# Attention layer: squares folded in two, one ones-product per sum of squares, the norm chain and the last score pairs a slot later

## The reference, cut to what matters

```python
def rms_norm(x, g):
    xf = x.astype(jnp.float32)
    y = xf * lax.rsqrt(jnp.mean(xf * xf, axis=-1, keepdims=True) + EPS)
    return (y * g.astype(jnp.float32)).astype(x.dtype)
...
    q = rms_norm(q, q_norm_g[:, None, :])
    k = rms_norm(k, k_norm_g[:, None, :])
    ...
    q, k = partial_rope(q, cos, sin), partial_rope(k, cos, sin)
```

## Time and profile before

| | |
|---|---|
| median of 3 runs | 2274.46 us (2269.77 to 2276.57) |
| the profiled execution, its own time | 2273.7 us |
| its span, first to last instruction | 2272.0 us |
| busy over the span: PE, PEld | 2232.2 us (98%), 1869.4 us (82%) |
| busy over the span: DVE, ACT, POOL | 1395.7 us (61%), 1231.3 us (54%), 398.0 us (18%) |
| mean granted clock of TensorE | 0.998 |
| attention heads | about 1081 to 2187 us of the span; from the second on, the scaled copies of one head start 137.5 us after those of the head before |
| weight loads of the attention heads | 80 of 512 KB, median 3.9 us from issue to landing |

### The profile page before, as it was taken

How to read it: one execution, slowest core, us unless ns; L and a number is a source line. 1 busy time by engine, 2 the same in 40 slices (tenths; PEclk the granted TensorE clock), 3 DMA queues, 4 the chain that set the end, 5 groups by cost and what they waited for, 6 DMA issues and landing times. The chain is left out here.

```text
span 2272.0 us, 31343 instructions
## 1 busy us (share of the span) xinstructions
PE 2232.2 (98%) x11056; PEld 1869.4 (82%) x11056; DVE 1395.7 (61%) x2594; ACT 1231.3 (54%) x2509; POOL 398.0 (18%) x672
## 2 busy tenths in 40 slices
PE   7999999999999999999999999999999999999999
PEld 5788888888888888777888888888888888888887
DVE  5867758585867665586745738366482755728451
ACT  5656656566666665555545455454555545455440
POOL 2435162533525160560000000000000000000000
PEclk9999999999999999999999999999999999999999
DMA  4212231322222245586111121121111211121241
GB/s 144 56 45 65 72 84 46 82 47 71 50 68 61 59 106 179 189 264 202 56 38 57 29 57 47 38 65 39 48 38 40 64 47 40 37 64 49 92 175 60
DMA packets 301726, 174.26 MB, mean 77 GB/s; under 512 B 97228, under 2 KB 284004, under 8 KB 301572
## 3 DMA queue, kind: packets, MB, share of 16 engines
q1 hardware_dynamic: 301572, 172.26, 26.6%
HBM read 143.66 MB, written 28.56 MB: 76 GB/s over the span
## 5 line engine op out<-in xcount | busy, mean ns | idle before, releaser
L390 PE MATMUL b_front<-g_h_lo,wa_w_hi 128*128 128x512 f32 x2064 | 827.3, 401 | 0.0
L390 PE MATMUL b_front<-g_h_hi,wa_w_hi 128*128 128x512 f32 x2064 | 821.9, 398 | 5.4 <-PEq L1563 3.0
L390 PE MATMUL b_front<-g_h_hi,wa_w_lo 128*128 128x512 f32 x2064 | 823.9, 399 | 0.0
L390 PEld LDWEIGHTS b_front<-g_h_hi,wa_w_hi 128*128 128x128 f32 x2064 | 388.6, 188 | 82.5 <-issue 6.2
L390 PEld LDWEIGHTS b_front<-g_h_lo,wa_w_hi 128*128 128x128 f32 x2064 | 388.5, 188 | 76.7 <-issue 0.2
L390 PEld LDWEIGHTS b_front<-g_h_hi,wa_w_lo 128*128 128x128 f32 x2064 | 388.4, 188 | 76.1 <-issue 0.5
L2215 ACT ACTIVATE b_acc<-b_front,g_gains 128x512 f32<-128x512 f32 x96 | 66.2, 689 | 300.3 <-DVE p_qk L2534 201.1
L1287 DVE SCALAR_TENSOR_TENSOR a_acc<-a_x_raw,a_hw,a_acc 128x512 f32<-128x512 f32 x192 | 156.9, 817 | 6.6
L2405 DVE TENSOR_TENSOR wa_w_lo<-wa_raw,wa_w_hi 128x1024 fp32r<-128x1024 f32 x79 | 95.6, 1210 | 106.2 <-ACT wa_w_hi L2161 106.2
L779 POOL TENSOR_TENSOR a_bt<-a_bd,a_bx 128x112 f32<-128x112 f32 (+29 forms) x248 | 116.7, 471 | 213.7 <-DMA a_bd<-u_tiles 194.9
L782 POOL TENSOR_TENSOR a_bx<-a_bx,a_bt 128x112 f32<-128x112 f32 (+29 forms) x248 | 131.4, 530 | 19.4
(11 more groups left out here) (355 smaller groups left out, 4074.0 us busy)
## 6 DMA issues: line engine op xcount, KB each, us to landing
wa_raw<-in_b_w_in_dram SPq DMA_DIRECT2D x80, 512.0 KB, 3.9
wa_raw<-in_a_w_in_dram SPq DMA_DIRECT2D x48, 512.0 KB, 4.5
p_w_raw<-in_a_w_out_dram SPq DMA_DIRECT2D x40, 512.0 KB, 4.1
a_out<-a_og SPq DMA_DIRECT2D x64, 128.0 KB, 1.9
a_zx<-inverse_tiles SPq DMA_DIRECT2D x16, 384.0 KB, 4.4
p_a_raw<-a_out SPq DMA_DIRECT2D x40, 128.0 KB, 4.9
u_tiles<-a_u SPq DMA_DIRECT2D x8, 512.0 KB, 3.2
a_bd<-u_tiles SPq DMA_DIRECT2D x32, 128.0 KB, 3.6
```

Source lines behind the costliest of these rows:

```text
L390: last = pe.matmul(out, w[:, k, :], a[:, k, ks], start=(n == 0), stop=(n == 23))
```

## The change

The squares of the lower 64 dimensions stay where they were (`sg`), those of the upper 64 are written to the lower partitions of a second buffer (`sq_up`); DVE adds the two, so 64 rows of sums of two squares are left. ACT rounds them to their high part in partitions 0 to 63 of `sq_rows`, and DVE writes the low part into its partitions 64 to 127. One product with the matrix of ones then sums all of it. Moved: the high part from ACT's delay 3 to 4, behind Ln and Exp of the half before; the low part on DVE from ahead of the rotation to behind the sine product; the product of ones from 5 to 6, Ln and Exp from 6 to 7, the norm product from 7 to 8; score pairs 8 to 11 from slots 5 to 8 to slots 6 to 9. `evac` now counts when the second square is done. The semaphore `carrier` is shared by both layers, which changes no wait.

```diff
-PAIRS_LATE0 = 5
+PAIRS_LATE0 = 6
...
-        sq_hi = m_.sb("sq_hi", [P, HALF], F32R)
-        sq_lo = m_.sb("sq_lo", [P, HALF], F32R)
+        sq_rows = m_.sb("sq_rows", [P, HALF], F32R)
+        sq_up = m_.sb("sq_up", [P, HALF])
+        low_rows, up_rows = slice(0, P // 2), slice(P // 2, P)
...
-                        act.activation(sg[:, half], proj[half][:, :], ACT.Square).then_inc(evac, 1)
-                        act.wait_ge(evac, head * B_HALVES + (q + 1))
-                        act.wait_ge(nsum, head * 12 + (q + 1))
-                        act.activation(sq_hi[:, :], sg[:, half], ACT.Copy).then_inc(sq_high, 1)
+                        act.wait_ge(sq_low, head * 12 + q)
+                        act.activation(sg[low_rows, half], proj[half][low_rows, :], ACT.Square)
+                        act.activation(sq_up[low_rows, :], proj[half][up_rows, :], ACT.Square).then_inc(evac, 1)
...
-                    for head, q in qk_at(m, n, s, 6):
+                    for head, q in qk_at(m, n, s, 7):
                         act.wait_ge(nsum, head * 12 + (q + 1 + 1))
                         act.activation(sg[:, q % 2], side[:, :], ACT.Ln, scale=1.0 / DK, bias=EPS).then_inc(rss, 1)
...
+                    for head, q in qk_at(m, n, s, 4):
+                        act.wait_ge(sq_sum, head * 12 + (q + 1))
+                        act.wait_ge(nsum, head * 12 + (q + 1))
+                        act.activation(sq_rows[low_rows, :], sq_up[low_rows, :], ACT.Copy).then_inc(sq_high, 1)
...
-                    for head, q in qk_at(m, n, s, 5):
+                    for head, q in qk_at(m, n, s, 6):
                         pe.wait_ge(sq_low, head * 12 + (q + 1))
...
-                        pe.matmul(side[:, :], r.ones_r[:, :], sq_hi[:, :], start=True, stop=False)
-                        pe.matmul(side[:, :], r.ones_r[:, :], sq_lo[:, :], start=False, stop=True).then_inc(nsum, 1)
+                        pe.matmul(side[:, :], r.ones_r[:, :], sq_rows[:, :], start=True, stop=True).then_inc(nsum, 1)
...
                     for head, q in qk_at(m, n, s, 4):
-                        dve.wait_ge(sq_high, head * 12 + (q + 1))
-                        dve.tensor_tensor(sq_lo[:, :], sg[:, q % 2], sq_hi[:, :].bitcast(F32),
-                                          ALU.subtract).then_inc(sq_low, 1)
+                        dve.wait_ge(evac, head * B_HALVES + (q + 1))
+                        dve.tensor_tensor(sq_up[low_rows, :], sq_up[low_rows, :], sg[low_rows, q % 2],
+                                          ALU.add).then_inc(sq_sum, 1)
...
                         dve.tensor_tensor(swap[:, :], swap[:, :], rope_tables.sin[:, cols], ALU.mult).then_inc(ropes, 1)
+                        dve.wait_ge(sq_high, head * 12 + (q + 1))
+                        dve.tensor_tensor(sq_rows[up_rows, :], sq_up[low_rows, :], sq_rows[low_rows, :].bitcast(F32),
+                                          ALU.subtract).then_inc(sq_low, 1)
                         dve.tensor_tensor(x, x, rope_tables.cos[:, cols], ALU.mult).then_inc(ropes, 1)
...
-                    for head, q in qk_at(m, n, s, 7):
+                    for head, q in qk_at(m, n, s, 8):
```

More of the change, by code:

```diff
@@ L430, in rows, with delta_heads @@
         return self.o_turned[k0 * P:k1 * P, cols].rearrange("(k p) n -> p k n", p=P)
-def delta_heads(nc, g, weights, proj, o_turned, front, o_stored, early):
+def delta_heads(nc, g, weights, proj, o_turned, front, o_stored, early, carrier):
     with ExitStack() as ctx:
@@ L537, in delta_heads @@
         totals = sem("totals")
-        carrier = sem("carrier")
         block = ctx.enter_context(nc.Block())
@@ L1889, in take, with attention_heads @@
         act.activation(self.cos[:, :], self.cos[:, :], ACT.Sin)
-def attention_heads(nc, r, rope_tables, weights, front, o_turned, final):
+def attention_heads(nc, r, rope_tables, weights, front, o_turned, final, carrier):
     with ExitStack() as ctx:
@@ L1954, in attention_heads @@
         o_stored = final.o_stored
-        carrier = sem("carrier")
+        sq_sum = sem("sq_sum")
         block = ctx.enter_context(nc.Block())
@@ L2586, in program @@
             o_stored = banks.sem("o_stored")
+            carrier = banks.sem("carrier")
             early = EarlyProjection(g, weights, a_w_out[0], a_out)
-            delta_heads(nc, g, weights, proj, a_out, front, o_stored, early)
+            delta_heads(nc, g, weights, proj, a_out, front, o_stored, early, carrier)
             rope_tables = RopeTables(nc, layer, g, positions)
@@ L2593, in program @@
             final = FinalProjection(nc, layer, g, weights, front, b_w_out[0], b_out, x1, out[0])
-            attention_heads(nc, g, rope_tables, weights, front, b_out, final)
+            attention_heads(nc, g, rope_tables, weights, front, b_out, final, carrier)
             final.run(g)
```

## The result

The changed kernel takes 2305.68 us (median of 4 runs, 2304.69 to 2306.72), the kernel before 2274.77 in the same session: a ratio of 1.0143, with a 95% interval of 1.0129 to 1.0157. It is slower, as forecast, but by 31 us where 13 were forecast, and it lies above the range of 2268 to 2300. The profiled execution took 2306.11 us, with a span of 2304.4.

What follows compares the result with a forecast made beforehand. PE is full but a serial ACT-DVE loop is slower; lengthened to 6.80 us, it loses 4.6 to 4.7 per head against 2.72 + 0.22 saved: +12 over seven heads, +1 in the first, 2287.5 us, range 2268 to 2300.

Steps and rivals of the forecast that it cites:

- the loop: Serial ACT and DVE chain closed through both acc buffers: 6.36 us before, 6.80 after, 6.40 behind group 0's norm product.
- The removed matmuls: On PE, one product of ones fewer per half, 96 of 0.227 us: 21.8 us saved, 2.72 per head.
- Added on ACT: Second square enters the loop, high part leaves: DVE's first step 1.71 us after the scaled copy instead of 1.88; alternatively 1.81.
- Added on DVE: Inside the loop, add and low part replace the old low part, one step more: +0.61 us.
- its pessimistic end: Upper length for the ACT and DVE loop with the norm product of groups 1 and 2: 6.90 us instead of 6.80.
- The room at q = 10: Slack regained while score pairs slow PE from q = 7 to 10: PE 23.2 us, loop 21.8, room 1.4.
- The first head: No earlier output work or lag; 3.8 us lost against 2.72 saved: +1.1 us.
- the room at q = 1: First head's slack before the product of ones must wait: 7.48 us less 0.2, 4.39 and 0.05, so 2.8.
- its rival: Freed matmuls are kept, stalls per head below 2.9 us by a loop of about 6.4: 2253 us, chance 0.13.
- Late score pairs: Join about 2.7 us later, covered by ACT's idle 2.63 us, nothing charged; rival adds 8 to 16 us, chance 0.05.
- Half price for 64 partitions: Alternative to full price: steps on half the partitions take half the time, loop shorter by some 0.3 for each of three.
- Clock: Granted clock stays 1.00 in the heads; rival: it falls after the longest gaps, 15 us on top, 2302, chance 0.04.

Runs made afterwards that it cites:

- x4_three_buffers: Changed kernel with three acc buffers, the lower square in spare swap partitions and only Ln waiting for the norm product: 2257.13 us, ratio 0.9923 to the kernel before.
- the control: Kernel before the change, given the same third acc buffer: 2272.18 us, ratio 0.9991, heads 137.23 us apart.
- x6_both_in_place_full: Changed kernel with second square and low part each staying in their partitions, product of ones still over 128 rows, sum incomplete: 2282.03 us, ratio 1.0035 to before.
- b2_before_late_pairs: Kernel before the change with only score pairs 8 to 11 moved to slots 6 to 9: 2275.46 us, ratio 1.0002.
- x5_pool: Changed kernel with the addition of the squares and the low part moved from DVE to POOL: 2318.86 us, ratio 1.0196 to the kernel before.

## Why the prediction was right in sign and short in size

- **What bounds the kernel, and the loop: right, and shown.** The stalls came at q = 4 to 7 and 11 and at pair 8, ended by the low part and the norm product. Opening the loop with all of the added work left in gives 2257 us. Its matmuls, its score pairs and its granted clock in the heads are those of the changed kernel.
- **The removed matmuls: right.** 2.72 us per head; `x4_three_buffers` keeps 1.74 of them beside the control (137.23 - 135.49), and its stall at q = 4 is the rest (1650.95 - 5.67 - the product before, at 1644.41: 0.87, and the restart).
- **The step that failed: the pitches priced under "Added on ACT" and "Added on DVE".** I took 0.49 between two reads of PSUM for the second square (1.71 us to DVE's first step) and 0.61 for each step beside the low part, pitches of neighbours that stay in their partitions. Measured: 1.81, 0.72 and 0.71. The loop is 7.10 us instead of 6.80. The alternative that the prediction worked out for ACT, 0.59 and 1.81, was the right one; for DVE it had none on that side, and its pessimistic end for the loop was 6.90. With both steps in place the loop is 6.76.
- **From the loop to the heads.** From the product of q = 3 (1670.68) to that of q = 7 (1697.85) PE took 27.17 us and needs 4 x 5.665 = 22.66: 4.5 lost where 3.4 were forecast. The room at q = 10: the low part of that half was ready 0.7 us ahead of its product, not 1.4. From q = 10 to q = 11 it took 7.12: 1.45 lost, forecast 0.4. From that product to pair 8 it took 4.53, of which 3.97 are the restart and the matmuls: 0.56 lost, forecast 0.5. With a restart of 0.1 behind each of the three, 6.8 instead of 4.6 to 4.7. Against 2.94 saved that is +3.9 per head and 27 us over seven heads, where the spacing shows 7 x 3.86 = 27.0.
- **The first head.** 133.08 us instead of 128.61 to the next head, +4.5 where +1.1 was forecast. It has six rounds of growth up to q = 7, so the same 0.3 us make 1.8; the room at q = 1 was 2.2 us and not 2.8; q = 11 is as in the other heads, 1.0 more. Together 3.4.
- **Why 0.3 us cost 18.** Each round that lags behind PE adds the error once: four up to q = 7, and four more up to q = 11 once the room at q = 10 is used up. From `x6_both_in_place_full` to the changed kernel, 0.34 x 8 = 2.7 us per head; the spacing says 141.34 - 138.62 = 2.72. The prediction knew this slope and gave the loop a tenth of a microsecond either way. (By its own terms a tenth is 0.8 us per head, 6.4 in all: its 2298 at the upper end should be 2294, and the stalls of 2.9 us at which its rival begins belong to a loop of 6.6, not 6.4.) The range was too narrow because that tenth covered one engine and one step, and three pitches had the same unseen property.
- **Late score pairs: right** (`b2_before_late_pairs`). **Half price for 64 partitions: refuted**, as the durations show. **Clock: right.** It stayed at 1.00, the 2.4 GHz level, over the heads with 72 idle stretches of at most some 0.7 us each. The Trainium skill, TensorE: Matmul & The Clock Gate, section "A second HAM failure mode: psum-queue depth-cycling", which I weighed there, tells of a clock that swings with many short idles; the trace doesn't show it at this length of gap. In `x5_pool` the granted clock does fall, behind an idle time of 3.16 us. Its windows around that stall (columns as in the earlier trace rows):

```profile
1684.00:1687.00 3.00, 0.21 (x1) 0.21 (x2) 2.97 (x5) 0.92 (x2) 2.74 (x1) 0.94 0.05 12
1687.00:1691.00 4.00, 4.00 (x12) 3.14 (x13) 2.96 (x4) 2.81 (x5) 2.21 (x2) 0.62 0.42 122
1691.00:1695.00 4.00, 4.00 (x19) 3.31 (x18) 1.56 (x4) 2.19 (x4) 1.41 (x2) 1.00 0.01 4
```

What stays open: what in the chip makes a change of partitions between neighbouring steps cost their overlap. That it is this change, and not the move, rests on ACT's seven Exps and on the addition of `x4_three_buffers`; no run was made for it alone, and for the low part on DVE the two can't be told apart.

## What to carry to other kernels

When PE is full, a change that takes matmuls away has to be judged by the closed loops of the other engines, not by their busy shares. Write the loop down step by step, compare it with PE's new period, and multiply each tenth by the number of rounds that lag. Give a step whose kind no row shows, here one that starts at other partitions than its neighbours, its full duration and no overlap with either neighbour as its pessimistic end. If the loop is the longer one, opening it is worth more than the removed work: here a third buffer alone turned +31 us into +2, and with another place for the lower square into -18.

## What the runs showed of the hardware

- A step that reads one set of 64 partitions and writes the other takes about as long as one in place (0.69 us beside 0.67 on DVE, 0.60 beside 0.58 on ACT), but the overlap with its neighbours can be lost. On DVE the pitches are 0.72 and 0.71 us beside 0.61 and 0.60; on ACT 0.59 and 0.62 beside 0.47 and 0.48.
- On ACT the overlap is lost between two reads of PSUM that start at different partitions: behind the second square an Exp in SBUF follows after 0.49 to 0.50 us, and the Ln of PSUM behind it after 1.07 instead of 0.95.
- On DVE and ACT, 64 partitions cost as much as 128: 0.68 us for the addition beside 0.69 for the old low part, 0.58 for a square beside 0.59.
- A product of ones over 64 rows among matmuls over 128 rows costs PE some 0.4 us more than one over 128 (it starts 0.37 us after its neighbour, the next two 0.42 and 0.33 after it, instead of 0.227 each), with no wait shown.
- After a wait for another engine, the second matmul starts 0.34 us after the first instead of 0.227 (before: 1676.19 to 1676.53).
- POOL needs 1.50 us in the mean, and 1.26 at least, for an addition of 64 x 512 fp32 elements that DVE does in 0.68, and while both read two tiles each, both slow down, up to 1.78 us for DVE's cosine product and 3.77 for POOL's low part.
